# Spreading routing work over three places in each attention unit, and normalizing one unit later, in a one-core encoder step

## The reference

```
h = x + concat(sparse_attention, forgetting_attention) @ w_out
h = h + memory_attention(rms_norm(h) @ w_mem_q, mem_k, mem_v) @ w_mem_o      # 4 heads of 256, 256 memory tokens
h = h + peer_ffn(rms_norm(h))                                                # top-16 of 128 x 128 experts, 8 heads
```

## Time and profile before

| what | value |
|---|---|
| median of 3 runs | 3981.93 us (3975.78 to 3982.06) |
| the profiled execution, its own time | 3975.78 us |
| its span, first to last instruction | 3973.9 us |
| PE busy | 3465.6 us, 87% |
| DVE busy | 2470.7 us, 62% |
| POOL busy | 1956.6 us, 49% |
| ACT busy | 1068.1 us, 27% |
| mean granted TensorE clock | 0.943 |

### The profile page before, as it was taken

The page is one execution under the profiler, slowest core; times in us unless marked ns, Lnnn a source line. Parts: engine busy times, 40 slices in busy tenths (PEclk is TensorE's granted clock), DMA queues, the critical chain, the costliest instruction groups (busy, mean ns, idle before and its releaser), DMA issues. The chain is left out here.

```text
span 3973.9 us, 50433 instructions
## 1 busy us (share of the span) xinstructions
PE 3465.6 (87%) x17237; PEld 2509.2 (63%) x17237; DVE 2470.7 (62%) x5777; ACT 1068.1 (27%) x2008; POOL 1956.6 (49%) x1478
## 2 busy tenths in 40 slices
PE   7888888897998888866898889868769999999998
PEld 4446666667798776655676767655546556656665
DVE  3779894232222377789999999998733444434434
ACT  1214444352121232212232222223322222222222
POOL 0000000003124344677787888865366776877773
PEclk9889899999998999988999999989989999999999
DMA  2000100004213444898999999989898999999996
GB/s 116 10 33 18 34 12 6 11 0 146 105 43 138 137 138 161 310 372 324 377 394 373 390 387 394 378 315 388 329 346 340 356 349 357 376 350 366 377 375 232
DMA packets 328009, 960.17 MB, mean 242 GB/s; under 512 B 33680, under 2 KB 83736, under 8 KB 326272
## 3 DMA queue, kind: packets, MB, share of 16 engines
q0 software_dynamic: 156672, 570.49, 36.7%
q1 hardware_dynamic: 166352, 372.22, 26.1%
q10 hardware_dynamic: 4784, 14.82, 1.0%
HBM read 862.73 MB, written 94.68 MB: 241 GB/s over the span
## 5 line engine op out<-in xcount | busy, mean ns | idle before, releaser
L1533 PE MATMUL m_ps<-m_xh_flat,m_wh 128*128 128x512 f32 x3072 | 761.7, 406 | 153.5 <-POOL m_wh L1523 151.6
L1533 PEld LDWEIGHTS m_ps<-m_xh_flat,m_wh 128*128 128x128 f32 x3072 | 589.0, 195 | 320.6 <-POOL m_wh L1523 195.3
L2491 PE MATMUL e_y_ps<-e_wh,e_vh 128*128 128x512 f32 x3072 | 740.0, 397 | 45.2 <-DVE e_wh L2615 34.0
L2491 PEld LDWEIGHTS e_y_ps<-e_wh,e_vh 128*128 128x128 f32 x3072 | 572.3, 189 | 256.8 <-issue 128.5
L981 POOL CAST m_wh<-raw 128x1024 fp32r<-128x1024 f32 x40 | 42.6, 1066 | 1159.0 <-issue 914.9
L1018 PE MATMUL m_ps<-m_xh_flat,m_wh 128*128 128x272 f32 (+1 forms) x2880 | 499.0, 334 | 73.8 <-DVE m_xh_flat L1074 20.3
L1018 PEld LDWEIGHTS m_ps<-m_xh_flat,m_wh 128*128 128x128 f32 x2880 | 438.0, 195 | 129.4 <-issue 42.7
L2174 POOL DMA_INDIRECT e_rows<-in_v,eid x448 | 447.7, 999 | 125.8 <-issue 114.1
L2575 POOL TENSOR_TENSOR e_vh<-raw,e_vh 128x1024 fp32r<-128x1024 f32 x128 | 309.8, 2423 | 216.9 <-ACT e_vh L2517 214.0
L2654 DVE TENSOR_TENSOR oT<-e_y_ps,oT 128x512 f32<-128x512 f32 x256 | 173.5, 691 | 330.6 <-PE e_y_ps L2491 261.9
L1523 POOL TENSOR_TENSOR m_wh<-raw,m_wh 128x1024 fp32r<-128x1024 f32 x128 | 307.5, 2403 | 56.6 <-ACT m_wh L1518 54.6
(11 more groups left out here) (319 smaller groups left out, 5254.4 us busy)
## 6 DMA issues: line engine op xcount, KB each, us to landing
raw<-in_ut SPq DMA_DIRECT2D x128, 512.0 KB
raw<-in_v SPq DMA_DIRECT2D x126, 512.0 KB
s_hid<-flat SPq DMA_DIRECT2D x128, 256.0 KB
xrow<-s_hid SPq DMA_DIRECT2D x126, 256.0 KB
s_gate<-g_stage SPq DMA_DIRECT2D x3, 8192.0 KB, 53.2
raw<-in_w_pq SPq DMA_DIRECT2D x32, 512.0 KB
e_gate<-s_gate SPq DMA_DIRECT2D x32, 512.0 KB
gh<-s_gate SPq DMA_DIRECT2D x32, 512.0 KB
```

Of the source, the lines that this page charges most:

```text
L1533: mm = pe.matmul(self.ps[:, n % 2, 0:ND], self.uh[:, at % 2, a, k * P:(k + 1) * P], self.xd[:, b, k, :], start=(k == 0 and o == 0), stop=( ...
L2491: mm = pe.matmul(y_ps[:, o, 0:TD], vh[:, n % SLOT, a, m * P:(m + 1) * P], wh[:, SLOT - 1 - n % SLOT, b, g * TD:(g + 1) * TD], start=(c == ...
```

## The change

`attend_dve` is written anew, for both passes. `normalize(u + 1)` no longer stands ahead of `row_max(u + 2)` and `split_result(u - 1)`; each turn of the loop now begins with `normalize(u)`. Where routing work is interleaved (second pass only) it now stands in three places of a unit instead of one, each with 1.8 in place of 2.4. In the PKQ products the amount is 4.4 in place of 5.4.

```
@@ attend_dve
         self.row_max(dve, 0)
         self.row_max(dve, 1)
-        self.normalize(dve, 0)
         for u in range(n):
-            if u + 1 < n:
-                self.normalize(dve, u + 1)
+            self.normalize(dve, u)
             if beside:
                 beside()
             if u + 2 < n:
                 self.row_max(dve, u + 2)
+            if beside:
+                beside()
             if u >= 1:
                 self.split_result(dve, u - 1)
+            if beside:
+                beside()
         self.split_result(dve, n - 1)
@@ route, vector engine
-            mx.attend_dve(dve, lambda: progress.fill(2.4))
+            mx.attend_dve(dve, lambda: progress.fill(1.8))
...
             for n in range(PKQ, END):
-                progress.fill(us + 1.0)
+                progress.fill(us)
```

## The result

The changed kernel takes 4025.4 us (median of four runs, 4024.4 to 4027.9) where the kernel before takes 3978.9 beside it: ratio 1.0113, 95% interval 1.0098 to 1.0128, so 39 to 51 us slower. 4027 was forecast. Twelve further executions of it took 4014.6 to 4029.8 us. The profiled execution has a span of 4023.0 us, 49 more than the 3973.9 of before.

The account below looks back on a forecast made before the run. PE was taken to bound both attentions, DVE the ten chunks behind END. The terms 20 + 26.5 + 15 - 5.5 - 7.5 = 48.5 us slower gave 4027 us, 8-in-10 range 4006 to 4048.

Parts of the forecast that it names:

- The chain in the first attention: First attention: the new order closes a chain of 6.29 us a unit against 3.95, adding 20 us.
- The chain in the second attention: Second attention: the same chain with routing work in it, 54.1 us from turn 0 to 7 against 27.0, so +26.5.
- The seven steps: Second attention, turn 0 to turn 7: the times from each turn to the next, together 54.1 us.
- The clock: Both attentions: a lower PE clock adds 0.8 us in each of eight steps and 1.2 in seven, 15 us.
- the 6.4 in the sum: First attention: the clock's part, 0.8 us for each of its eight steps.
- What comes back: PKQ and the stretch from END to dot 128: time regained, -5.5 us and -7.5 us.
- the stated bound of 8: END to dot 128: the gain was bounded by 0 and -8 us, with -7.5 counted.
- the sixteen pieces: Behind END: sixteen L1744 routing pieces, 4.3 us, can run inside DVE's idle 16 us.
- That the clock stays up: Rival for both attentions: no clock loss, 33.5 us more than before, 4009 to 4015; chance 0.22.
- The gathers' collision: Rival in the second attention: 11 more gathers each hold a TENSOR_SCALAR for their length, +10 us, 4037; chance 0.07.
- That dot 128 gives all back: Rival behind the ten chunks: ACT's 34.0 us wait with PKQ's 12.3 could return 46, ending at 3975 to 3990; chance 0.04.
- that the order costs nothing: Rival in the first attention: the chain does not bind PE, it stays at 44.5 us, kernel 3978 to 3985; chance 0.02.

Follow-up runs that it names:

- the second execution: The changed kernel with no further edit, profiled once more: 4020.1 us.
- the order alone: Kernel before with normalize(u) at the head of each turn in both passes, routing amounts as before (2.4 once a unit, 5.4 in PKQ): 4023.8 us, ratio 1.0121.
- the second execution of before: The kernel before, unchanged, profiled once more: 3971.0 us.
- ahead of the split: Kernel before with normalize(u + 1) moved behind row_max(u + 2) but ahead of split_result(u - 1), routing work as before: 3977.4 us, ratio 1.0002.
- the run with PKQ alone: Kernel before with only the amount in the sixteen PKQ products changed, 4.4 in place of 5.4: 3974.2 us, ratio 0.9989.
- with 5.2: Kernel before with 5.2 in place of 4.4 in the 24 other second-pass products and 4.4 in PKQ: 3969.3 us, ratio 0.9990.
- with 4.8: Kernel before with 4.8 in place of 4.4 in the 24 other second-pass products and 4.4 in PKQ: 3958.5 us, ratio 0.9964.
- the amounts alone: Kernel before with its old order, but three places of 1.8 in a unit and 4.4 in PKQ: 3981.3 us, ratio 1.0013.

## Why the prediction was right

**The chain in the first attention** was the main step, and it came as worked out. A round was 6.29 us in the prediction and is 6.31, with 2.14 us of idle time before L1118 where "about 2.1" stood. Turn 0 to turn 9 is 54.8 us (1107.91 to 1162.75) against 33.1 before (1108.80 to 1141.86), so 21.8 more. Of these 1.7 are one round at half clock, so 20.1 belong to the order, where 20 were forecast. The steps had small errors in both directions: the two units whose scores have 32 rows take 6.6, and the last turn, which has no scores ahead of it, 4.5.

**The chain in the second attention.** The seven steps were forecast as 7.2, 8.6, 8.1, 7.4, 8.4, 8.5 and 5.9. They are 7.1, 10.1, 9.7, 9.1, 8.4, 8.7 and 6.5, 59.7 us for 54.1 without the clock. One step in the changed kernel, PE and DVE:

```profile
1499.33 1.12 PE L1118 MATMUL m_a_ps<-con,flat 128*128 128x128 f32 x4 [4.74 <-DVE flat L1208]
1500.23 2.96 PE L1108 MATMUL m_ps<-m_mk_p,m_q_flat 128*128 128x256 f32 x8
1503.03 1.95 PE L1129 MATMUL m_a_ps<-m_pt,m_mv_p 128*128 128x128 f32 x16
...
1506.12 0.69 DVE L1190 TENSOR_TENSOR m_xh_flat<-m_a_ps,m_xh_flat 128x512 fp32r<-128x512 f32 x1
1506.72 0.28 DVE L1751 MAX8 r_v<-oT 128x8 f32<-128x128 f32 x1
...
1508.54 0.14 DVE L1204 RECIPROCAL m_rinv<-m_rsum 128x2 f32<-128x2 f32 x1
1508.72 0.62 DVE L1208 TENSOR_SCALAR flat<-flat,m_rinv 128x256 f32<-128x256 f32 x2
1509.39 1.12 PE L1118 MATMUL m_ps<-con,flat 128*128 128x128 f32 x4 [4.41 <-DVE flat L1208]
```

Between the split and the reciprocal stand the four pairs of L1751 and L1752, 1508.54 - 1506.72 = 1.82 us on the path, as forecast. Turn and scores are at half clock, 1.12 and 2.96 us for 0.66 and 1.89. The candidate sums were priced at 2.2 us and took 0.89 (one row of L1761 at 1543.66). The experiments split the 32.7 us by which turn 0 to turn 7 grew, each with the clock that it had, into 16.4 for the order (43.4 - 27.0), 6.9 for the further amount where it stands ahead of the split (50.3 - 43.4), and 9.4 for the third place (59.7 - 50.3).

**The clock** was mis-sized. In the first attention one round of eight had the lower clock (half of full speed, 1.2 of 2.4 GHz), in its turn and scores, and lasted 1137.04 to 1145.02, 7.98 us for 6.31:

```profile
1137.04 1.05 PE L1118 MATMUL m_a_ps<-con,flat 128*128 128x128 f32 x4 [2.13 <-DVE flat L1208]
1137.88 3.22 PE L1108 MATMUL m_ps<-m_mk_p,m_q_flat 128*128 128x256 f32 x8
1140.94 1.95 PE L1129 MATMUL m_a_ps<-m_pt,m_mv_p 128*128 128x128 f32 x16
```

That is 1.7 us for the 6.4 in the sum. The granted clock from 1137.04 to 1140.94 is 0.56, and 1.00 from 1107.9 to 1137.0; that of the whole stretch is 0.94 (0.95 in the second execution), where "well below 0.96" was said. With the order alone the first attention had it in three rounds and ended 3.2 us later than the changed kernel's. In the second attention it fell to 0.82 and lay upon most turns; the measured steps exceed the forecast ones by 5.6, or by 6.9 with the candidate sums at what they took, against 8.4. So the term of 15 should have been 7 to 9. It was the idle share of the round, 2.3 of 6.3 us, that I had put beside the ten chunks, and this case shows the same share with 0.94 in one place and 0.83 in the other.

**What comes back.** PKQ gave 6.2 us (4.4 in the second execution) for 5.5 forecast, against the first execution of before. In the second execution of before PKQ is 5.0 us shorter with nothing changed, so this total alone shows little. The row of waits is as told, the long one kept and the rest nearly gone:

```profile
PE m_ps L1018 <- POOL m_wh L997: 7.3, 2, 7.1
```

All eleven profiled executions together separate the two. Without the longest, PE's waits for the split in PKQ add up to 4.0 to 7.0 us in the four with 5.4 (before twice, the order alone, ahead of the split) and to 0.2 to 2.5 us in the seven with 4.4. The longest lies between 3.9 and 7.6 us in the four and between 2.0 and 7.4 in the seven. So the lower amount takes away the short waits, as forecast (1.5 of 6.9 was to remain); the long one varies with either amount, from 5.4 to 3.9 between the two executions of before. Of the 8.6 us that these waits fell in the run with PKQ alone, 5.7 are short waits and 2.9 the long one; the 9.7 us with 5.2 against 2.7 with 4.8 are mostly the long one.

END to dot 128 gave 9.8 us in both executions for 7.5 forecast, past the stated bound of 8. The mechanism was right in its source and wrong in one detail, the place of the sixteen pieces (L1746 in the changed kernel):

```profile
1731.09 0.28 DVE L1746 MATCH_REPLACE8 oT<-r_v,r_s 128x128 f32<-128x128 f32 x1
...
1750.65 1.22 DVE L1659 CUSTOM_DVE_ANT_0 m_ring<-m_ring,m_row_ps 128x1024 f32<-128x1024 f32 x1 [19.29 <-DMA m_ring<-in_u,eid]
...
1848.94 1.03 ACT L2014 ACTIVATE m_row_ps<-xrow 128x1024 f32<-128x1024 f32 x1 [26.80 <-DVE gh L1659]
```

They do not run inside the idle time behind END. They are over before END (1732.8), and DVE then stands still for 19.3 us, where it stood 16.0. So the whole of them is gone from the path to dot 128, and with them the three dots, 7.9 us. The rest was not in the sum. Some short routing pieces of DVE that stand beside a split on POOL end only 0.1 to 0.2 us behind it, and which pieces stand there depends on the order. The same instruction in the kernel before, with its split, and in the changed kernel, with none beside it:

```profile
1773.53 2.86 DVE L1788 TENSOR_SCALAR r_sab<-r_place 128x128 f32<-128x128 f32 x1
1773.94 2.35 POOL L1523 TENSOR_TENSOR m_wh<-raw,m_wh 128x1024 fp32r<-128x1024 f32 x1
...
1814.93 0.25 DVE L1790 TENSOR_SCALAR r_sab<-r_place 128x128 f32<-128x128 f32 x1
```

Three such pieces between END and dot 128 take 2.82, 2.86 and 1.84 us before, and three others 1.66, 1.76 and 1.62 in the changed kernel, 2.5 us less. ACT's wait fell from 34.0 to 26.8. From PKQ to dot 128 the order alone moves no work and regains 1.7; the amounts alone move the same work and regain 15.1, and the changed kernel 16.0 (14.2 the second time). Behind END alone it is 0.3, 10.1 and 9.8, where the executions of before part by 0.2. That the return comes from the amounts, and not from the longer attention, is shown by this pair.

**The sum.** First attention 26.4 forecast and 23.4 measured, second 34.9 and 32.6 up to PKQ, PKQ -5.5 and -6.2, to dot 128 -7.5 and -9.8, behind it 0 and +9.0 (-0.6 the second time). At dot 128 the forecast was 48.3 and the two executions are 41.0 and 43.5 us behind their own start of the first attention. The medians are 46.5 apart. Within the profiled execution part of the agreement is luck: a clock term some 7 us too large stands against 9 us that arose where both orders are the same.

**The rivals.** That the clock stays up would have given 4009 to 4015; it stayed up in most of the first attention and not in the second. The gathers' collision (the third rival, though the prediction calls it the last) is refuted by rows. POOL issues a gather beside the scaling of unit 7:

```profile
1551.19 0.62 DVE L1208 TENSOR_SCALAR flat<-flat,m_rinv 128x256 f32<-128x256 f32 x2
...
1551.35 1.01 POOL L2099 DMA_INDIRECT m_ring<-in_u,eid  x1 [1.26 <-DVE gh L1659]
```

The scaling takes 0.62 us, as without a gather, and so it is for all three units of this attention that have a gather beside their scaling, in both executions of the changed kernel. It is the three gathers that take a little longer there, 1.00 to 1.01 us for 0.94. The largest effect on a scaling in any run is 0.1 us: two beside a gather take 0.71 and 0.72 us in the run with the normalization ahead of the split. The contention on VectorE's side of which the Trainium skill speaks ("GPSIMD Engine Reference", section "Key points") is not seen for this pair in the changed kernel. Beside a split it is another matter: the 2.74 us of the TENSOR_SCALAR in the earlier trace rows are 0.23 us where no split runs (L1788 at 1418.77). That dot 128 gives all back fell at 16 of 56 us, and that the order costs nothing at the first idle 2.14 us.

## What to carry to other kernels

When a loop's step is moved behind another on an in-order engine, write down what each then waits for and follow it round: here one place further (behind the row maximum) cost 1.7 us once and nothing in the later units, and two places further cost 2.36 us in each unit, because only the second closed a ring through three engines. Work that is laid into such a ring is free ahead of the instruction that waits, as long as it is shorter than the wait, and costs its full length behind it. And work moved ahead in time pays only at the wait that it shortens: look for that wait first (here ACT's for dot 128), and raise the amounts where the engine has idle time, in small steps: of 4.4, 4.8 and 5.2 in the 24 products, with 4.4 in PKQ, only 4.8 could be told from the kernel before.

## What was not expected of the hardware

A stretch in which PE repeats 4.2 us of work and 2.1 us of idle time did not hold one clock. In four executions with the same instructions in the first attention, one, one, three and one of its rounds were at half clock (some 1.7 us more each) and the others at full clock. And executions of one kernel part from each other: the two of before by 5.0 us in PKQ alone, with the same instructions in it, and the two of the changed kernel by 9.6 us behind dot 128. A DVE instruction of 0.23 us took up to 2.86 us where a split of 2.4 us ran on POOL, and ended 0.1 us behind the split's end.
